# Experts' weights in 4 KB runs, token gather and scatter in fp32r

## The reference

```python
def grouped_moe(h, router_w, router_bias, w_gate, w_up, w_down):
    scores = sigmoid(einsum('nd,de->ne', h, router_w))
    ...  # best group of 4 experts by biased score, best 2 experts in it
    gates = sel / sum(sel)
    dense_gates = einsum('nk,nke->ne', gates, one_hot(idx, 16))
    y = 0
    for e in range(16):
        a = silu(h @ w_gate[e]) * (h @ w_up[e])      # 1024 -> 512
        y = y + dense_gates[:, e:e + 1] * (a @ w_down[e])   # 512 -> 1024
    return y

# second block, layer l
h = layer_norm(ALPHA * h + attention(h), ln1_g[l], ln1_b[l])
h = layer_norm(ALPHA * h + grouped_moe(h, ...), ln2_g[l], ln2_b[l])
```

## Time and profile before

| | us |
|---|---|
| median of 3 runs | 1879.68 (1878.11 to 1882.62) |
| profiled execution | 1881.95 |
| its span, first to last instruction | 1880.2 |
| first block and attention of layer 1 | 0 to 1108 |
| experts of layer 1: first gate_up to last scatter | 1151.3 to 1395.8 |
| experts of layer 2: first gate_up to last scatter | 1618.9 to 1863.7 |
| PE busy, DVE busy, ACT busy (shares of the span) | 86%, 50%, 33% |
| moved by DMA | 427.65 MB |

### The profile page before, as it was taken

How to read it: one execution, slowest core, us unless ns; L and a number is a source line. 1 busy time by engine, 2 the same in 40 slices (tenths; PEclk the granted TensorE clock), 3 DMA queues, 4 the chain that set the end, 5 groups by cost and what they waited for, 6 DMA issues and landing times.

```text
span 1880.2 us, 19165 instructions
## 1 busy us (share of the span) xinstructions
PE 1619.5 (86%) x7639; PEld 1123.2 (60%) x7639; DVE 943.0 (50%) x1394; ACT 616.0 (33%) x871; POOL 29.5 (2%) x59
## 2 busy tenths in 40 slices
PE   2889879999699987999796967999969696899995
PEld 1677757788577766888585754333328575433331
DVE  5896667854587766554555653111135574211102
ACT  1335633442334444443243711111124371111111
POOL 2000000000000000000100000000000000000000
PEclk8999998999799988999897978999989797899998
DMA  9685346855587443655553065999965306599994
GB/s 331 228 284 183 134 157 224 310 182 179 176 294 264 140 134 121 230 177 189 173 173 123 1 225 194 387 386 386 387 250 183 123 1 245 194 387 386 386 387 184
DMA packets 199019, 427.65 MB, mean 227 GB/s; under 512 B 8056, under 2 KB 16432, under 8 KB 198928
## 3 DMA queue, kind: packets, MB, share of 16 engines
q1 hardware_dynamic: 195344, 417.43, 63.0%
q0 software_dynamic: 3360, 8.87, 1.7%
q10 hardware_dynamic: 224, 0.07, 0.0%
HBM read 425.30 MB, written 1.05 MB: 227 GB/s over the span
## 4 chain that ended last, share of the span: by engine, by line
PE 40%; SPq 13%; DVE 7%; DMA 2%; ACT 1%; issue 1%; DVEq 0%
SPq L680 13%; PE gp L1934 12%; PE gp L2106 8%; PE gp L2267 8%; PE gp L2252 2%; DMA raw_deep<-in_exp_w_down 2%; PE mp L2298 1%; PE mp L2125 1%; PE mp L2164 1%; PE mp L2175 1%; PE mp L2174 1%; PE mp L2183 1%; DVE stats L1547 1%; DVE x L1563 1%; PE mp L2196 0%
## 5 line engine op out<-in xcount | busy, mean ns | idle before, releaser
L1200 DVE TENSOR_TENSOR wlo<-raw,whi 128x2048 fp32r<-128x2048 f32 (+1 forms) x132 | 289.6, 2194 | 225.2 <-ACT whi L779 223.9
L779 ACT ACTIVATE whi<-raw 128x2048 fp32r<-128x2048 f32 (+1 forms) x132 | 242.1, 1835 | 370.5 <-PE gp L1934 207.2
L1934 PE MATMUL gp<-whi,xt_hi 128*128 128x512 f32 (+1 forms) x800 | 318.9, 399 | 31.6 <-DVE xt_lo L1249 14.1
L1934 PE MATMUL gp<-wlo,xt_hi 128*128 128x512 f32 (+1 forms) x800 | 312.8, 391 | 0.0
L1934 PE MATMUL gp<-whi,xt_lo 128*128 128x512 f32 (+1 forms) x800 | 312.4, 391 | 0.0
L1934 PEld LDWEIGHTS gp<-whi,xt_hi 128*128 128x128 f32 x800 | 155.5, 194 | 71.8 <-DVE wlo L1200 16.8
L1934 PEld LDWEIGHTS gp<-whi,xt_lo 128*128 128x128 f32 x800 | 155.3, 194 | 31.3
L1934 PEld LDWEIGHTS gp<-wlo,xt_hi 128*128 128x128 f32 x800 | 155.5, 194 | 29.3 <-issue 0.2
L1805 DVE TENSOR_SCALAR pr<-slots,key,dg 128x128 f32<-128x128 f32 x64 | 19.3, 344 | 261.0 <-PE gp L2288 261.0
L1110 DVE SCALAR_TENSOR_TENSOR acc<-raw,cact,acc 128x1024 f32<-128x1024 f32 x69 | 88.5, 1282 | 3.4 <-DMA raw<-in_w_ada 2.0
L1127 DVE TENSOR_TENSOR wlo<-raw,whi 128x2048 fp32r<-128x2048 f32 (+3 forms) x36 | 68.3, 1907 | 41.2 <-ACT whi L925 40.6
(11 more groups left out here) (379 smaller groups left out, 2436.9 us busy)
## 6 DMA issues: line engine op xcount, KB each, us to landing
raw<-in_w_in SPq DMA_DIRECT2D x60, 1024.0 KB, 5.7
raw<-in_w_ada SPq DMA_DIRECT2D x42, 1024.0 KB, 5.4
raw_deep<-in_exp_w_down SPq DMA_DIRECT2D x36, 1024.0 KB, 14.2
raw_deep<-in_exp_w_gate SPq DMA_DIRECT2D x30, 1024.0 KB, 14.2
...
```

Source lines behind the costliest of these rows:

```text
L779: act.activation(slot(whi, s % SPLIT, units, cols), slot(raw, g % RAW, units, cols), ACT.Copy).then_inc(hi_done.sem, 1)
L1200: dve.tensor_tensor(slot(wlo, s % SPLIT, units, cols), slot(raw, g % RAW, units, cols), slot(whi, s % SPLIT, units, cols).bitcast(F32), AL ...
L1934: mm = pe.matmul(gp[:, q % 2, t, 0:wide], a[:, chunk, ts], w[:, unit, c0:c0 + wide], start=first and n == 0 and m == 0, stop=last and n == ...
```

## The change

The kernel after does the following.

- **Runs of 4 KB.** A gate or up unit gives partition p the rows 2p and 2p+1 of each block of 256 rows, which lie side by side in memory; a unit is then two 4 KB runs per partition. A down unit is 256 rows with all 1024 columns, also two 4 KB runs. `down` waits for its units one after the other.
- **Paired columns.** For the tokens to fit the gate and up rows, the layer norm ahead of the experts writes `x` with even and odd columns in separate blocks (`in_pairs`, `by_pairs`), in four instructions with stride 2 for two; the closing sum turns it back, also in four. The router's weights are loaded to match, by four DMAs for one.
- **Gather in fp32r, for eight experts at once.** ACT writes `h_hi`, the rounded `x`, DVE `h_lo`, the rest, both ahead of the routing's end. `gather` makes one chunk of 128 inputs for eight experts (512 columns) with four fp32r matmuls: two tiles, high and low. Eight chunks stand ahead of the first expert, the other eight behind experts 0 to 7. `pick` is made in two instructions for a group, that of the first group ahead of the branch.
- **Scatter in fp32r.** ACT copies `ag` first, then the turned gates to `back_gates` and with the same instruction sums each row to `gate_of`. DVE makes `back`, of ones and zeros, from it. ACT writes `yx_hi = gate * y`, rounded, DVE `yx_lo`, the rest. `scatter` is eight fp32r matmuls for four fp32 ones.

The diff, cut to its core:

```diff
-GROUP = 4
+GROUP = 8
...
             if i < 4:
-                return A["exp_w_gate_2" if i % 2 == 0 else "exp_w_up_2"][l, e, 4 * P * (i // 2):4 * P * (i // 2 + 1), :]
-            return A["exp_w_down_2"][l, e, :, COLS * (i - 4):COLS * (i - 3)]
+                rows = A["exp_w_gate_2" if i % 2 == 0 else "exp_w_up_2"][l, e, 4 * P * (i // 2):4 * P * (i // 2 + 1), :]
+                return rows.rearrange("(k p j) n -> p k (j n)", p=P, j=2)
+            return A["exp_w_down_2"][l, e, 2 * P * (i - 4):2 * P * (i - 3), :].rearrange("(k p) n -> p k n", p=P)
...
+                act.wait_ge(*h_ready.at2(l, 2))
+                for t in range(NT):
+                    act.activation(h_hi[:, t, :], x[:, t, :], ACT.Copy).then_inc(hh_ready.sem, 1)
...
-                    act.activation(back, bank_tr[:, T:2 * T], ACT.Copy).then_inc(back_ready.sem, 1)
-                    act.activation(ag, bank_tr[:, 0:T], ACT.Copy).then_inc(ag_ready.sem, 1)
+                    act.activation(ag[:, :], bank_tr[:, 0:T], ACT.Copy).then_inc(ag_ready.sem, 1)
+                    act.activation(back_gates[:, 0:T], bank_tr[:, T:2 * T], ACT.Copy, accum_out=gate_of[:, :]).then_inc(gate_ready.sem, 1)
...
-                    act.activation(yx, bank_y, ACT.Copy).then_inc(yx_ready.sem, 1)
+                    act.wait_ge(*gate_ready.at2(l, e + 1))
+                    act.activation(yx_hi[:, :], bank_y, ACT.Copy, scale=gate_of[:, :]).then_inc(yx_ready.sem, 1)
...
+                    if paired:
+                        for j in range(2):
+                            ins = dve.scalar_tensor_tensor(out=in_pairs(x[:, t, :], j), in0=by_pairs(cen[:, t, :], j), scalar=rr[:, t:t + 1],
+                                                           in1=by_pairs(lnw[:, 1, :], j), op0=ALU.mult, op1=ALU.add)
...
+                    dve.wait_ge(*hh_ready.at2(l, t + 1))
+                    dve.tensor_tensor(h_lo[:, t, :], x[:, t, :], h_hi[:, t, :].bitcast(F32), ALU.subtract).then_inc(hl_ready.sem, 1)
...
+                def way_back(e):
+                    dve.wait_ge(*gate_ready.at2(l, e + 1))
+                    dve.tensor_scalar(back[:, :], back_gates[:, 0:T], 0.0, None, ALU.is_gt).then_inc(back_ready.sem, 1)
+                def low_result(e):
+                    dve.wait_ge(*yx_ready.at2(l, e + 1))
+                    dve.scalar_tensor_tensor(out=yx_lo[:, :], in0=bank_y, scalar=gate_of[:, :], in1=yx_hi[:, :].bitcast(F32),
+                                             op0=ALU.mult, op1=ALU.subtract).then_inc(yl_ready.sem, 1)
...
+                    for t in range(NT):
+                        for h in (h_hi, h_lo):
+                            mm = pe.matmul(bank, h[:, t, P * c:P * (c + 1)], pick[:, t, :],
+                                           start=t == 0 and h is h_hi, stop=t == 1 and h is h_lo)
...
-                    side_by_side(e, 4, ag.rearrange("p (c n) -> p c n", c=4), 0, 0, (0, 1), bank_y, True, True)
+                    for i in range(4, 6):
+                        part, there, read, before = ring2(unit_at(e, i))
+                        pe.wait_ge(*there.at2(l, 16 * (before + 1)))
+                        w = parts_of(part, 2, D)
+                        for c in range(2):
+                            chunk = 2 * (i - 4) + c
+                            for n in range(2):
+                                mm = pe.matmul(bank_y[CAP * n:CAP * (n + 1), :], ag[:, CAP * chunk:CAP * (chunk + 1)], w[:, c, COLS * n:COLS * (n + 1)],
+                                               start=chunk == 0, stop=chunk == 3)
+                        mm.then_inc(read.sem, 1)
...
+                    pe.wait_ge(*yl_ready.at2(l, e + 1))
                     for t in range(NT):
-                        for half in range(2):
-                            rows = slice(CAP * half, CAP * (half + 1))
-                            mm = pe.matmul(mp[:, 2 * t + half, :], back[rows, P * t:P * (t + 1)], yx[rows, :], start=e == 0, stop=e == NE - 1)
+                        for y in (yx_hi, yx_lo):
+                            for half in range(2):
+                                rows = slice(CAP * half, CAP * (half + 1))
+                                mm = pe.matmul(mp[:, 2 * t + half, :], back[rows, P * t:P * (t + 1)], y[rows, :],
+                                               start=e == 0 and y is yx_hi, stop=e == NE - 1 and y is yx_lo)
```

249 lines of the change are left out of this document (152 added, 97 removed).

## The result

The changed kernel takes **1856.5 us** (median of 4 runs, 1854.5 to 1858.7) against 1881.0 us before (4 runs): ratio 0.9872, 95% interval [0.9854, 0.9890]. It is faster by 24.5 us, where 34.6 us were forecast; the time lies in the range, 11.5 us above the predicted one. The profiled execution has a span of 1855.1 us.

What follows compares the result with a forecast made beforehand. DMA was taken to bound the experts' stages, with PE 6 us behind. Per layer -15.5 - 1.8 - 0.4 + 0.4 + 0.0 = -17.3 us, -34.6 for both, giving 1845 us; 8 in 10 range 1836 to 1864 us.

Steps and rivals of the forecast that it cites:

- What bounds the kernel: Experts' stages: DMA decides with PE only 6 us behind, so speeding either alone can't gain much.
- the 224 us for PE alone: Experts' stage before the change: PE's own work from the first gate_up to down(14), summed as 224 us.
- The stream: Weight loads up to down(14): 4 KB runs raise DMA from 387 to 416 GB/s, -15.5 us per layer.
- the down's split: Down(14) computes with its first unit while the second lands, -1.8 us per layer.
- PE keeps up: Experts' stage: PE needs 197 us to down(14) against DMA's 214.8, so DMA decides from early on.
- its signs: Expected in the profile: PE waiting for DMA before most gate_up halves and downs from about the sixth expert, clock 1.00.
- The end: From the end of down(14) to the end of scatter(15): -0.4 us per layer, +1.0 if scatters run serially.
- Small steps: Work around the stage: closing sum +0.4 us, layer norm to first gate_up 0.0 us, per layer.
- The closing sum: After the experts: four halves for two wholes, 2.7 for 2.35 us, +0.4 us per layer.
- Ahead of the stage: From the layer norm's last step to the first gate_up: 0.0 us per layer, between -1 and +2.
- The rival of dearer small steps: Stride 2 at half speed, late h_lo and h_hi or a starved refill: +5.4 us a layer, 1856 us; chance 0.09.
- The sum: All terms together: -17.3 us per layer, -34.6 us for both layers, giving 1845 us.

Runs made afterwards that it cites:

- runs_2k: The changed kernel with the old weight layout (2 KB runs) and down waiting for both units at once; 1883.5 us, ratio 1.0010 to before.
- runs_only: The kernel before with only the 4 KB runs and what they need, gather and scatter still in fp32; 1873.0 us, ratio 0.9948 to before.
- stage_fill: The changed kernel with idle matmuls for PE ahead of gate_up(e, 0) from expert 9 on; 1854.1 us, ratio 0.9848 to before.

## Why the prediction was right and where it was wrong

**What bounds the kernel** held: DMA decides, PE is close behind, and neither alone gains much. runs_2k (nothing) and runs_only (7 us a layer) show it from both sides, and the 224 us for PE alone were 223.4.

**The stream, forecast -15.5 us a layer.** The step that failed is the rate: 416 GB/s, taken from one window of 4 us. The long stream has 409. By that, 82 x (2.71 - 2.564) = 12.0 us, 3.5 less. The trace of before has more of that place than the one window: 418 GB/s in the 4 us ahead of it, 407 in the 4 us behind it, 406 over 20 to 40 us. In the experts' stage of the changed kernel six such windows in a row show 409 or 410. The prediction read one window of an uneven stretch as the rate of a long stream. The prediction had a second number beside it: the Trainium skill's 408.7 GB/s ("DMA: Bandwidth & Descriptors", SWDGE vs HWDGE vs iDMA) for 1 MB loads in 4 KB rows. The trace now agrees with it, at 409. The same page's 512 B for line rate (Specifications) is not what this stream shows: 387, 409 and 421 GB/s at 2, 4 and 8 KB. With the down's split (-1.8), 13.8 us were to be had to the end of down(14), and the trace has 219.7 for 233.9, -14.2 us.

**PE keeps up** held in its numbers: a scatter takes 1.13 us (1.1 forecast, the row halves do run side by side), a gather part 1.1 us from start to start (0.91 forecast), an early expert 13.6 us for 15.2. The waits came later and fewer than its signs had them: one per expert from expert 10 on, and not in front of most halves and downs from about the sixth. What failed is the sentence that the clock would stay at 1.00 because PE had waited as much before. Its longest waits were 1.8 us then and are 2.8 us now, and a share of waiting says nothing on how long each is. The Trainium skill ("TensorE: Matmul & The Clock Gate", Why this matters for your kernels) advises against idle gaps between bursts of matmuls for this very reason. The trace agrees for this wait (0.57 behind 2.7 us), and the prediction had left the rule out. In the stream the low clock cost nothing (stage_fill), because PE had the time.

**The end, forecast -0.4 us.** Measured +3.1 us from the end of down(14) to the closing sum (13.7 for 10.6). Of this 2.85 us are down(15) at half clock, which no term had. The rest, +0.25, differs from -0.4 mainly because `yx_lo` lengthens the scatter's wait from 0.70 to 1.67 us, 0.97 twice and not 0.77; 0.2 us more are the turning of `ax`, partly at half clock (0.66 us for 0.46). The scatters gave 0.8 each, as worked out.

**Small steps.** The closing sum was +0.1 for +0.4. Ahead of the stage it was -0.4 and -0.9 us for 0.0: the layer norm's step +0.5 (0.3 forecast), `h_lo` +1.1 (1.2 forecast), and pick and gather gave the rest. The rival of dearer small steps has the right time, 1856 us, by a cause that didn't occur.

**The sum.** Forecast 17.3 a layer; measured 11.7 and 12.2 up to the closing sum. The stream's rate took 3.5 us and the clock at the end 2.9 us from the forecast, and the small terms together gave some 1 us more than forecast. With 409 GB/s and the fallen clock the prediction's own sum would have given -17.3 + 3.5 + 2.9 = -10.9 a layer, 1858 us; that the measured 1856.5 is nearer is the small terms' doing.
